# Two column tiles of 64 slots for the matmuls of an expert block, in place of one of 128

## The reference, cut to what matters

```python
def swiglu(t, wg, wu, wd):
    return (jax.nn.silu(t @ wg) * (t @ wu)) @ wd
# 64 experts, 8 per token; w_gate, w_up: (64, 1024, 256), w_down: (64, 256, 1024)
def one_block(args):
    tok, e = args
    xb = t_pad[tok]                      # the tokens that chose expert e
    return swiglu(xb, wg[e], wu[e], wd[e])
y = zeros.at[buf_tok].add(out * buf_w)   # back to the tokens, weighted
```

## Time and profile before

| | |
|---|---|
| three runs | 1493.2, 1493.64, 1497.81 us; median 1493.64 |
| profiled execution | a span of 1495.0 us; no time of its own beside the span was recorded |
| PE busy in the span | 1411.4 us (94%), 4809 matmuls and 4809 weight loads |
| share of the chain that ended last | PE 80%, DMA 10%, DVE 4% |
| expert blocks | from about 664 us to the end |

### The profile page before, as it was taken

One profiled execution on the slowest core, in us unless ns is written; L12 is line 12 of the kernel. 1 busy time (PEld: TensorE's weight loads), 2 busy tenths in 40 slices (PEclk: granted clock), 3 DMA queues, 4 the chain that ended last, 5 costly groups with the idle time before them and its releaser, 6 DMA issues.

```text
span 1495.0 us, 16946 instructions
## 1 busy us (share of the span) xinstructions
PE 1411.4 (94%) x4809; PEld 739.8 (49%) x4809; DVE 536.7 (36%) x1408; ACT 222.3 (15%) x506; POOL 217.5 (15%) x237
## 2 busy tenths in 40 slices
PE   5938999999999999989999999999999999999996
PEld 4524444444788444444454445444445444455443
DVE  3406472500565223463333333333333333333332
ACT  4000000110555011200111111111111111111110
POOL 0000000000220000001222222222222222222222
PEclk9958999999999999999999999999999999999999
DMA  9864661221100220508999999999999999999992
GB/s 298 266 122 147 232 225 57 67 102 56 57 0 0 113 92 28 197 13 294 325 316 310 320 314 310 315 325 316 319 311 297 311 297 305 315 308 297 310 300 68
DMA packets 230412, 323.54 MB, mean 216 GB/s; under 512 B 20042, under 2 KB 188018, under 8 KB 230386
## 3 DMA queue, kind: packets, MB, share of 16 engines
q1 hardware_dynamic: 207440, 284.68, 56.7%
q0 software_dynamic: 21488, 36.25, 10.7%
q10 hardware_dynamic: 1458, 2.27, 0.4%
HBM read 321.02 MB, written 42.99 MB: 243 GB/s over the span
## 4 chain that ended last, share of the span: by engine, by line
PE 80%; DMA 10%; DVE 4%; another core or an unknown queue 4%; SPq 1%; issue 1%; ACT 0%; POOL 0%; DVEq 0%; POOLq 0%; ACTq 0%
PE PS L1424 29%; PE PS L1166 15%; PE PS L1440 13%; DMA R_Z<-w_up_e 7%; PE PS L1295 4%; PE PS L1324 4%; PE PS L1414 3%; DVE R_A L745 2%; PE PS L1228 2%; PE PS L1334 2%; PE PS L1204 2%; PE PS L1216 1%; DMA R_T<-ada_w 1%; DMA R_Z<-ada_w 1%
## 5 line engine op out<-in xcount | busy, mean ns | idle before, releaser
L1424 PE MATMUL PS<-R_Z,R_G 128*128 128x512 f32 x1104 | 486.3, 593 | 3.8 <-DMA R_Z<-w_up_e 3.7
L1424 PEld LDWEIGHTS PS<-R_Z,R_G 128*128 128x128 f32 x1104 | 208.6, 190 | 270.9 <-issue 255.7
L1166 PE MATMUL PS<-R_W,R_HT 128*128 128x512 f32 x640 | 277.4, 595 | 1.1 <-DVE R_HT L768 1.1
L1440 PE MATMUL PS<-R_Z,R_G 128*128 128x512 f32 x552 | 255.6, 606 | 0.6 <-issue 0.6
L1166 PEld LDWEIGHTS PS<-R_W,R_HT 128*128 128x128 f32 x640 | 122.3, 191 | 153.1 <-issue 151.8
L503 POOL DMA_INDIRECT out<-R_G,ridx x69 | 109.3, 1583 | 599.8 <-issue 569.2
L1039 DVE TENSOR_TENSOR R_G<-R_G,PS 128x256 f32<-128x256 f32 x69 | 29.1, 421 | 445.8 <-ACT R_G L686 445.8
L1440 PEld LDWEIGHTS PS<-R_Z,R_G 128*128 128x128 f32 x552 | 99.9, 191 | 100.8 <-issue 100.7
L691 ACT ACTIVATE R_G<-PS 128x256 f32<-128x256 f32 x69 | 26.5, 384 | 710.8 <-PE PS L1431 694.3
L1049 DVE SCALAR_TENSOR_TENSOR R_G<-PS,slx,MOD 128x512 f32<-128x512 f32 x138 | 103.6, 750 | 52.7 <-PE PS L1440 46.7
L491 POOL DMA_INDIRECT R_G<-h_rows,gidx x73 | 76.0, 1041 | 99.1 <-DVE slx L1027 52.4
(11 more groups left out here) (209 smaller groups left out, 969.3 us busy)
## 6 DMA issues: line engine op xcount, KB each, us to landing
R_Z<-w_gate_e SPq DMA_DIRECT2D x69, 1024.0 KB, 8.2
R_Z<-w_up_e SPq DMA_DIRECT2D x69, 1024.0 KB, 11.9
R_Z<-w_down_e SPq DMA_DIRECT2D x69, 1024.0 KB, 12.8
R_W<-w_in SPq DMA_DIRECT2D x10, 2048.0 KB, 8.5
R_T<-ada_w SPq DMA_DIRECT2D x18, 1024.0 KB, 7.2
R_Z<-ada_w SPq DMA_DIRECT2D x6, 1024.0 KB, 16.2
R_Z<-w_out SPq DMA_DIRECT2D x1, 4096.0 KB, 12.8
bias_rows<-R_G POOLq DMA_DIRECT2D x1, 2560.0 KB, 57.3
```

The costliest lines, as they stand in the source:

```text
L1166: ins = mm(PS[:, t, :], HT[:, k, P * t:P * t + P], WR[:, b, k, :], start=k == 0, stop=k == KD - 1)
L1424: ins = mm(PS[:, b, :], XT[:, b, k, :], WGU[b][:, k, :], start=k == 0, stop=k == KD - 1)
L1440: ins = mm(PS[:, 2 + half, :], AT[:, b, k, :], WDN[b][:, k, 512 * half:512 * half + 512], start=k == 0, stop=k == 1)
```

## The change

In `gate_up` and in `down` each matmul is issued as two. The first takes slots 0 to 63: the stationary operand is cut to its first 64 columns, and the output goes to PSUM partitions 0 to 63 of the same bank. The second takes slots 64 to 127 and writes partitions 64 to 127. Both stream the same weights, all 512 columns. The loop over the two stands inside the loop over k, so that the halves alternate. The semaphore goes up with the very last matmul, as before. Nothing else is touched: not the transposes, the buffers, the DMAs, the other engines, nor the shared expert.

```diff
                 for k in range(KD):
-                    ins = mm(PS[:, b, :], XT[:, b, k, :], WGU[b][:, k, :], start=k == 0, stop=k == KD - 1)
+                    for c in range(0, P, 64):
+                        ins = mm(PS[c:c + 64, b, :], XT[:, b, k, c:c + 64], WGU[b][:, k, :],
+                                 start=k == 0, stop=k == KD - 1)
                 ins.then_inc(s_gu, 1)
...
                     for k in range(2):
-                        ins = mm(PS[:, 2 + half, :], AT[:, b, k, :], WDN[b][:, k, 512 * half:512 * half + 512],
-                                 start=k == 0, stop=k == 1)
+                        for c in range(0, P, 64):
+                            ins = mm(PS[c:c + 64, 2 + half, :], AT[:, b, k, c:c + 64],
+                                     WDN[b][:, k, 512 * half:512 * half + 512], start=k == 0, stop=k == 1)
                     ins.then_inc(s_dn, 1)
```

## The result

Four runs of the changed kernel took 1501.39 to 1503.28 us, median **1502.61 us**; four of the kernel before, among them those shown above, 1493.2 to 1497.81, median 1494.07 us. The ratio is 1.0048, with a 95% interval of 1.0034 to 1.0062: slower by 8.5 us, and by the interval between 5.1 and 9.3 us. The forecast was 1541.5 us, with a range from 1520. The sign was right; the size was not.

What follows compares the result with a forecast made beforehand. The prediction took PE to bound the kernel, with DMA a close second. Per block 0.429 + 0.065 + 0.20 = 0.694 us, x 69 = 48 us, gave 1493.6 + 47.9 = 1541.5 us, range 1520 to 2225.

Steps and rivals of the forecast that it cites:

- What bounds the kernel: Expert blocks: PE bounds at 11.58 us a block, DMA a close second; weights come 3.5 us early.
- Overlap of the two tiles: Touched matmuls of gate_up and down: both column tiles run at once, adding no full stream; with lag, chance 0.50.
- The order, +0.429 us a block: Each block's run of down and gate_up: tile 1 trails tile 0 by T, so 24 T becomes 25 T.
- if each tile had its own order, it would be 0: Rival for the blocks: a queue per tile, no lag, only width changes cost, 14 us, 1507 us; chance 0.06.
- the rival of 1764 us: Tiled matmuls: weight loads cannot pass a waiting matmul and lose cover, 3.92 us a block, 270 us; chance 0.13.
- Each added start, +0.065: Tiled matmuls of a block: each start after the other tile's costs 0.0027 us, 24 times, 0.065 us a block.
- Changing the width, +0.20: Two tile-width changes a block, into 64 columns before down and out after gate_up: 0.10 us each.
- the tail of 0.165 us: Width changes, if each drains the engine: full matmul tail paid twice, 0.33 us a block, sum 1550 us.
- Who waits for it: Work behind gate_up and down on other engines, and weight DMAs: semaphores up to T later, costed at nothing.
- The serial case: Rival for the tiled matmuls: second half waits for the first, 10.51 us a block, 725 us, 2219 us; chance 0.26.

Runs made afterwards that it cites:

- experiment 3: The kernel before, with down weights loaded for the first two blocks only and then reused: 1490.32 us, ratio 0.9959 to the kernel before.
- experiment 5: The kernel before, with the two transposes of turn_act issued twice in each block: 1505.3 us, ratio 1.0055 to the kernel before.
- experiments 6 to 8: The changed kernel with its half matmuls reordered; records of one tile in a row in gate_up: sixteen 1859.97 us, four 1505.38 us, eight 1631.28 us.
- experiment 6: The changed kernel with all half matmuls of slots 0 to 63 before those of 64 to 127, in gate_up and each half of down: 1859.97 us.

## Why the prediction was wrong, step by step

*What bounds the kernel.* Right in kind, PE with DMA close behind, but "a longer PE block costs its full length" failed. The weights that came 3.5 us early in the block that I read were late in nine others, and those cost 6.7 us in the profiled run. The prediction had the row of waits and took 3.7 us as too small to count; summed over 66 blocks (11.682 for 11.58) they were 6.7 us, half of the 13.6 us by which PE's work grew. Taking the waits away gained 5.9 us (experiment 3), and 15.2 us of added transposes cost 8.6, so that 6.6 were given back (experiment 5).

*Overlap of the two tiles.* Right: 485.6 us busy for 486.3.

*The order, +0.429 us a block.* This is **the step that failed**: "b0 stands behind a1, so it starts at T, beside a1". It was 30 of the 48 us. Tile 1 starts with a0, and `gate_up` takes 16 T and the block no 25th, since a matmul record passes up to three waiting ones of the other column tile (experiments 6 to 8). The text named the condition, "if each tile had its own order, it would be 0", and gave that case 0.06. Its 1507 us less the 6 to 7 us of waits given back comes near the measured 1502.6. Its picture, a queue for each tile, is not right either: a fourth record is not passed. The Trainium skill, TensorE: Matmul & The Clock Gate, Part 3, says that matmuls start and end in program order; the starts here disagree, 911.42 us in experiment 6 being the clearest. The rule there for loads, which gave the rival of 1764 us, disagrees too: half-width loads of 137 ns run in pairs under matmuls of the same rows, and no T became longer.

*Each added start, +0.065.* Nothing that shows: four tiles cost what two do.

*Changing the width, +0.20.* Measured 0.04 + 0.15 = 0.19. The sum is right by luck, its parts are not: 0.10 was set for each. Into half width behind short matmuls is nearly free, and the price behind a 512-column matmul is 0.15 to 0.19. The Trainium skill, TensorEngine Tiling (Array Packing), Key Properties, says that a change of mode drains the engine. The end of a `gate_up` in the changed kernel:

```profile
911.76 1.46 PE L1425 MATMUL PS<-R_Z,R_G 128*64 128x512 f32 x6
...
913.15 0.33 PE L1433 MATMUL PS<-cst,R_G 128*128 128x128 f32 x1
```

The last pair starts 2 T behind 911.76, at 912.62, and the transpose 0.52 us behind it, for 0.43 without a change. So the engine does wait, by some 0.1 us, but not to the modelled end of the matmuls, 0.592 us behind their start; the other 0.05 to 0.1 us come with the next matmul. That this is a drain, or that its price is the tail of 0.165 us, is not shown.

*Who waits for it.* Right: no new wait of ACT or DVE held PE up.

Put together: 0.19 to 0.20 us x 69 = 13.6 us, less the 6.7 us of waits given back in the profiled run, is 6.9 us, inside the interval of the measured 8.5 (5.1 to 9.3) and near the 6.1 of the spans. The forecast's 47.9 was this 13.6, the lag of 29.6 and the starts of 4.5, with nothing given back. The serial case, for which the range went up to 2225, did not occur for alternating tiles; tile after tile comes near it, at 1860.

## What to carry to other kernels

In these runs (f32, 512 columns) splitting a full-width matmul into column tiles that stream the same operand neither gained nor cost array time, but each change of tile width behind long matmuls cost 0.15 to 0.19 us. So tile a whole stretch or none, and count the changes. Column tiles overlap only if they alternate closely: four f32 records of one tile in a row (two matmuls of the code) were all but free, eight made `gate_up` a quarter longer, sixteen three quarters. And where a second resource is nearly full, read the mean period over all blocks and not one clean block: its difference is what a small cost or gain is first paid from.

## What the runs showed of the hardware that was not expected

- Matmuls of different column tiles start out of program order: three waiting f32 matmul records of one tile are passed, a fourth is not (28 T for two groups of 16, 20 T for groups of eight).
- Weight loads of different column tiles run side by side: two of 64 columns in 0.14 us, where one takes 137 ns.
- Four f32 tiles of 32 columns stream at once, each at the rate that one tile of 128 has: 64 records in 6.87 us, where 16 full-width ones take as long.
- A change from half to full width between long matmuls costs 0.19 us, from full to half 0.15 us, and behind short bf16 matmuls 0.04 us.
